# The feed-forward turn in the order gate, gate, value, value, way back, with the values copied out of PSUM by ScalarE

## The reference, cut to what matters

```python
def conv_ffn(xn, w_in, conv_w, conv_b, w_out, rows):
    a, v = _split(xn @ w_in, (D_FF, D_FF))
    if rows is None:
        a = dwconv_seq(a, conv_w[1])
    else:
        a = dwconv_grid(a, conv_w, rows)
    h = jax.nn.gelu(a + conv_b) * v
    return h @ w_out
```

## Time and profile before

| | us |
|---|---|
| median of three runs | 3967.95 (3964.62 to 3971.0) |
| span of the profiled execution | 3966.6 |
| TensorE matmul busy | 3448.7 (87% of the span) |
| VectorE busy | 1854.5 (47%) |
| GpSimd busy | 968.1 (24%) |
| ScalarE busy | 736.0 (19%) |

### The profile page before, as it was taken

The page is one execution under the profiler, slowest core; times in us unless marked ns, Lnnn a source line. Parts: engine busy times, 40 slices in busy tenths (PEclk is TensorE's granted clock), DMA queues, the critical chain, the costliest instruction groups (busy, mean ns, idle before and its releaser), DMA issues. The chain is left out here.

```text
span 3966.6 us, 49337 instructions
## 1 busy us (share of the span) xinstructions
PE 3448.7 (87%) x19579; PEld 3332.8 (84%) x19579; DVE 1854.5 (47%) x2483; ACT 736.0 (19%) x1381; POOL 968.1 (24%) x435
## 2 busy tenths in 40 slices
PE   8899999969799999999978889886868888888885
PEld 8788899959799999999977778776868888888885
DVE  2333332230755554555554244253365566655555
ACT  1333321121300010000004233232120000000000
POOL 1111122203123333333221212111212333233330
PEclk8898999979899999999988899898989999999997
DMA  3111121132211111111131010112310010110102
GB/s 155 39 52 51 51 74 51 61 101 73 86 54 57 59 69 58 63 53 53 53 105 56 27 42 24 38 36 79 112 39 32 32 37 33 36 37 32 37 32 96
DMA packets 86088, 225.58 MB, mean 57 GB/s; under 512 B 8000, under 2 KB 45120, under 8 KB 85872
## 3 DMA queue, kind: packets, MB, share of 16 engines
q1 hardware_dynamic: 44064, 163.16, 11.9%
q10 hardware_dynamic: 41936, 61.17, 4.5%
HBM read 193.89 MB, written 30.41 MB: 57 GB/s over the span
## 5 line engine op out<-in xcount | busy, mean ns | idle before, releaser
L712 PE MATMUL bank<-xh,wh 128*128 128x384 f32 x3888 | 1378.2, 354 | 225.3 <-DVE cc L2116 141.7
L712 PE MATMUL bank<-xl,wh 128*128 128x384 f32 x3888 | 1350.3, 347 | 0.0
L712 PE MATMUL bank<-xh,wl 128*128 128x384 f32 x3888 | 1346.1, 346 | 0.0
L693 POOL TENSOR_TENSOR wh<-raw,ones 128x1024 fp32r<-128x1024 f32 x206 | 420.2, 2040 | 2893.2 <-PE bank L712 1831.6
L712 PEld LDWEIGHTS bank<-xh,wh 128*128 128x128 f32 x3888 | 771.6, 198 | 258.5 <-DVE cc L2116 124.4
L712 PEld LDWEIGHTS bank<-xl,wh 128*128 128x128 f32 x3888 | 770.9, 198 | 0.5
L712 PEld LDWEIGHTS bank<-xh,wl 128*128 128x128 f32 x3888 | 768.7, 198 | 0.0
L2108 DVE SCALAR_TENSOR_TENSOR cc<-pad,cw,cc 128x1024 f32<-128x1024 f32 x352 | 573.8, 1630 | 6.9
L695 POOL TENSOR_TENSOR wl<-raw,wh 128x1024 fp32r<-128x1024 f32 x206 | 542.8, 2635 | 16.2
L712 PE MATMUL bank<-hh,wh 128*128 128x384 f32 x1056 | 373.0, 353 | 69.8 <-DVE y L2138 32.2
L2138 DVE TENSOR_TENSOR y<-y,bank 128x384 f32<-128x384 f32 x480 | 247.1, 551 | 278.1 <-PE bank L712 256.3
(11 more groups left out here) (231 smaller groups left out, 2622.2 us busy)
## 6 DMA issues: line engine op xcount, KB each, us to landing
raw<-in_w SPq DMA_DIRECT2D x206, 512.0 KB, 3.3
ada_w<-in_ada SPq DMA_DIRECT2D x80, 512.0 KB, 3.4
residual_scratch<-y ACTq DMA_DIRECT2D x9, 1536.0 KB, 5.9
xg<-residual_scratch ACTq DMA_DIRECT2D x9, 1536.0 KB, 7.9
xr<-mixer_scratch ACTq DMA_DIRECT2D x16, 576.0 KB, 3.8
front<-in_ada SPq DMA_DIRECT2D x16, 512.0 KB, 8.1
y<-in_x SPq DMA_DIRECT2D x1, 4608.0 KB, 19.6
mixer_scratch<-hout ACTq DMA_DIRECT2D x24, 192.0 KB, 1.9
```

The lines of the kernel that those rows point to most:

```text
L693: nc.gpsimd.tensor_tensor(wh[s][:, :], raw[s][:, :], ones[:, 0:1].broadcast_to([128, 1024]), ALU.mult).then_inc(w_hi[s], 1)
L712: return nc.tensor.matmul(out, lhsT, rhs, start=start, stop=stop)
```

## The change

TensorE's turn becomes gate 0, gate 1, value 0, value 1, and then the way back of the pair before; the host's order of the blocks and SyncE's pattern follow. ScalarE pads both gate tiles, and copies each value tile out of the three pj banks into a new SBUF tile `vs`, which frees the banks; `vs0` and `vs1` lie over tiles that only the norms use. VectorE does the 12 taps of tile 0, the 12 of tile 1, both products (now one instruction of 1152 elements each, from SBUF), then the 24 additions of the way back, then both parts hl. ScalarE writes hh once the way back, which reads the old hh, is over.

```diff
-            stream("ffn_b", FP - 1, "wawwwawawa")
+            stream("ffn_b", FP - 1, "wawawawaww")
...
                 with n.loop(pe, f"pe.ffn{layer}", FP - 1):
-                    project_all(slot())
-                    if with_ada:
-                        ada(0)
-                    down()
-                    for j in range(1, 4):
+                    for j in range(4):
                         project_all(slot())
                         if with_ada:
                             ada(j)
+                    down()
...
-            def dve_takes(s):
-
-                for c in range(2):
-                    n.next(pj_full[c])
+            def values(t, s):
+
+                for c in range(3):
+                    job(s, c)
+                    fn(vs[t][:, tg(c)], pj[c][:, 0:TG], COPY).then_inc(pj_free[c], 1)
                     n.next(pj_free[c])
-                n.next(w_used[s])
-                n.next(pj_free[2])
+                fn(tickw[:, t:t + 1], eps[:, :], COPY).then_inc(v_ready, 1)
...
             def upper(t):
-                act.wait_ge(pj_free[2], n.before(pj_free[2]))
+                act.wait_ge(h_ready, n.next(h_ready))
                 fn(hh[:, t, :], cc[t][:, :], COPY).then_inc(hh_ready, 1)
 
             def pair(with_down):
                 pads(0, slot())
+                pads(1, slot())
+                gelu(0)
+                values(0, slot())
+                gelu(1)
+                values(1, slot())
                 if with_down:
                     for _ in range(2):
-                        n.next(w_used[slot()])
-                gelu(0)
-                dve_takes(slot())
+                        s = slot()
+                        act.wait_ge(w_used[s], n.next(w_used[s]))
                 upper(0)
-                pads(1, slot())
-                gelu(1)
-                dve_takes(slot())
                 upper(1)
...
-            def value(t, s):
+            def value(t):
 
                 dve.wait_ge(gelu_done, n.next(gelu_done))
-                for c in range(3):
-                    full_ = w_used[s] if c == 2 else pj_full[c]
-                    dve.wait_ge(full_, n.next(full_))
-                    give(v.tensor_tensor(cc[t][:, tg(c)], cc[t][:, tg(c)], pj[c][:, 0:TG], ALU.mult), pj_free[c])
+                dve.wait_ge(v_ready, n.next(v_ready))
+                link(v.tensor_tensor(cc[t][:, :], cc[t][:, :], vs[t][:, :], ALU.mult), h_ready)
+
+            def rest(t):
                 dve.wait_ge(hh_ready, n.next(hh_ready))
...
                             give(v.tensor_tensor(dst, dst, mb[i][:, 0:TG], ALU.add), mb_free[i])
-                            if j % 2:
-                                conv_tap(0, j // 2)
...
             def pair(turn, with_down, column, saved=0):
                 set_taps(turn)
-                act_takes(slot())
+                for _ in range(4):
+                    act_takes(slot())
+                for t in range(2):
+                    for tap in range(12):
+                        conv_tap(t, tap)
+                value(0)
+                value(1)
                 if with_down:
                     down()
                 else:
-                    for tap in range(12):
-                        conv_tap(0, tap)
                     dve.wait_ge(x_saved, saved)
                     link(v.memset(y[:, :, :], 0.0))
-                value(0, slot())
-                act_takes(slot())
-                for tap in range(12):
-                    conv_tap(1, tap)
-                value(1, slot())
+                rest(0)
+                rest(1)
                 if column is not None:
                     conditioning(column)
```

More of the change, by code:

```diff
@@ L32 @@
               'conv_done': 2,
+              'h_ready': 2,
               'pj_free0': 4,
@@ L135 @@
               'mb_full3': 4,
-              'pj_free0': 2,
-              'pj_free1': 2,
-              'pj_free2': 2,
               'pj_full0': 4,
               'pj_full1': 4,
+              'v_ready': 2,
               'w_used0': 3,
@@ L398, in build @@
         tickv = sb("tickv", [128, 1])
+        tickw = sb("tickw", [128, 2])
         cond = sb("cond", [128, KT, 2])
@@ L427, in build @@
         ffn_scope = ExitStack()
+        values_scope = ExitStack()
+        vs = [sb(f"vs{t}", [128, T], scope=values_scope) for t in range(2)]
+        values_scope.close()
         sb("under_norm", [128, TG + KT * TG], scope=ffn_scope)
@@ L558, in build @@
             "conv_loaded a_padded conv_done gelu_done hh_ready hl_ready pads_clear")
+        v_ready, h_ready = sems("v_ready h_ready")
         mix_loaded, gates_logs, gates_rows, gates_exp, m_stored, cols_ready = sems(
@@ L2315, in ffn_blocks @@
     for p in range(FP):
-        blocks.append(a_(2 * p))
+        blocks += [a_(2 * p), a_(2 * p + 1), v_(2 * p), v_(2 * p + 1)]
         if p:
             blocks += down(p - 1)
-        blocks += [v_(2 * p), a_(2 * p + 1), v_(2 * p + 1)]
     return blocks + down(FP - 1)
```

## The result

The changed kernel takes 3715.3 us (median of four runs, 3711.9 to 3722.93); the kernel before took 3969.07 us in the same comparison. The ratio is 0.936, 95% interval 0.9347 to 0.9374. The forecast was 3714 us.

A forecast was written before the change was run, and what follows sets the result against it. TensorE bounds the kernel, losing 15.8 us a turn in layer 1 and 6.3 in layer 0. Savings of 175.2 and 79.2 us take 3966.6 to 3712.2; plus 1.35 for the median, told as 3714, range 3698 to 3748.

The forecast's parts named there:

- The length of a turn: TensorE's loop turn: 75.3 us in layer 1 and 82.4 in layer 0, where it was 91.0 and 88.8.
- The schedule inside a turn of layer 1: After TensorE ends gate 0: all taps over at 36 us (33 to 39), second product over at 40.8.
- The cover of 0.3 us: In layer 1's way back, the first addition frees bank mb0 at 41.4 us; TensorE's fifth group needs it at 41.7.
- The port: VectorE's product from SBUF shares ports with GpSimd's splits; if wl also went first, it would end at 43.2 us, costing 2.1.
- The third rival: TensorE's granted clock falls to 0.918 in the unbroken turns of both layers: 3855 us, chance 4%.
- The first rival: VectorE comes late to the additions of the way back, so TensorE waits there: 3735 to 3756 us, chance 17%.
- the prediction's own sign: The forecast is wrong if a turn of layer 1 takes more than 78 us or the clock falls in it.
- Weights: Each weight block is still split during TensorE's next block; layer 0 keeps 2.7 us of cover, so no wait.
- the second: Rival: conditioning transfers hold the weights in layer 0 and nothing is gained there: 3793 us, chance 4%.
- the fourth rival: VectorE's taps in a row keep GpSimd from splitting weights, 16.3 us in each of 20 turns: 4040 us, chance 2%.
- The last restarts: Before each layer's last way back TensorE waits for hh and hl: 7.2 us, once per layer, where 12.84 and 9.82 before.
- the start of layer 1: First pair: clearing y (7.74 us) moves behind the products and is covered; TensorE goes on at 2926.2 instead of 2936.41.

The follow-up runs named there:

- the thirds: The changed kernel with hh and hl made in six instructions of 384 columns each, the last way back starting per token group: 3716.9 us, ratio 0.9365.
- the order alone: The changed kernel without ScalarE's copies: VectorE multiplies out of the pj banks, product 0 ahead of the taps of tile 1; 3859.9 us, ratio 0.972.
- one copy: The changed kernel with only value 0 copied to SBUF; VectorE multiplies value 1 out of the pj banks in three instructions: 3710.8 us, ratio 0.9346.
- y cleared early: The changed kernel with VectorE clearing y between the two products in each layer's first pair, instead of behind them: 3703.8 us, ratio 0.9326.

## Why the prediction was right

- The length of a turn: 75.3 and 82.4 us forecast, 75.1 and 82.0 measured. The way of reading it, blocks of 12.48 us and groups of 1.056 where nobody holds TensorE, was good to 0.4 us.
- The schedule inside a turn of layer 1: taps over at 36, second product at 40.8, forecast; 35.8 and 40.7 measured. The cover of 0.3 us was real: 0.8 us of delay of the additions already made TensorE wait 0.5 us in each turn. Part of this is luck: the 36 rests on 16.2 us for the taps of tile 1, a value half way between two rows, and they took 15.9.
- The port: that a VectorE instruction with two SBUF inputs is served in turn with GpSimd's is seen at the second product (2.24 us against 1.36), behind wh and ahead of wl, which takes 3.40 us there; with a PSUM operand in its place the product takes 1.49 us and wl 2.40. The rule of the Trainium skill ("SBUF — State Buffer", section "SBUF: two separate sides"), exclusive for a whole instruction, also tells what the thirds did, and the trace agrees: the wait falls by a quarter only, since a small instruction (1.81 us beside wh, 0.56 alone) waits for wh too.
- The clock: 1.00 in turns of 75 us one behind the other, nine in layer 1. The third rival, less clock in unbroken work, did not come.
- The first rival, late additions, came in one turn only, the first of layer 1: 83.1 us with a clock of 0.50 behind the wait. By the prediction's own sign (more than 78 us, or the clock falls) that turn is a miss, in the other nine it holds.
- Weights: no wait of TensorE for GpSimd or for a transfer in either feed-forward part; the second and the fourth rival did not come.
- The last restarts: 7.2 us of wait each, measured 6.7.
- The term that was mis-sized is the start of layer 1: I put the clearing of y behind the products as covered. It is covered for TensorE's projections, but VectorE starts the taps of the first turn 7.2 us after gate 0 in place of 0.6, with 0.3 us of cover: 5.7 us of wait and some 2 with the slow clock. Between the restarts 2020.68 and 3886.16 lay 1865.5 us, and now 1696.9: a gain of 168.6, where I had 175.2. Layer 0 gave 82.7 where I had 79.2, since its turns are 0.4 us shorter; what follows the last restart gave 0.9. The sum, 252.2 for 254.4, is thus close partly because two errors have opposite signs.

What I did not forecast is how the gain divides. In the new order, by the experiments, ScalarE's copy of value 0 is the main part (149 us between the order alone and one copy; it also lets product 0 stand behind all taps), the place of the taps comes next (75 us with the copies there), and the copy of value 1 is nearly free of effect. In the old order no run takes the two copies apart; there it is the banks of value 1 that the next gate 0 needs.

## What to carry to other kernels

Work out how long one turn is where nobody holds the busiest engine, then walk through the turn to the first time at which each bank must be back; the mean share of a second engine says nothing of whether it is in time. A copy that frees a bank pays where the next projection needs that bank; where other banks come next, it can be left out. Look at the first and the last turn apart, since what is covered in the steady turn may come late there.

## What the runs showed of the hardware that was not expected

The 24 groups of a way back came 1.04 us apart in some turns and 1.06 in others, with the clock at 1.00 and no wait: the additions of the kernel after in two turns that follow each other.

```profile
3234.75 0.56 DVE L2141 TENSOR_TENSOR y<-y,bank 128x384 f32<-128x384 f32 x1 [0.49 <-PE bank L717]
3235.78 0.55 DVE L2141 TENSOR_TENSOR y<-y,bank 128x384 f32<-128x384 f32 x1 [0.48 <-PE bank L717]
...
3309.78 0.55 DVE L2141 TENSOR_TENSOR y<-y,bank 128x384 f32<-128x384 f32 x1 [0.51 <-PE bank L717]
3310.84 0.55 DVE L2141 TENSOR_TENSOR y<-y,bank 128x384 f32<-128x384 f32 x1 [0.51 <-PE bank L717]
```

In that kernel turns of 75.0 and 75.4 us alternate for most of layer 1; with thirds, or with y cleared early, all behind the first have 75.0, and with one copy all have 75.4. It is worth up to 4 us for ten turns. What decides it stays open: no run was made for it.

And a wait of TensorE costs more than its own length. Behind those of 3.4, 5.7, 6.4, 6.7 and 7.7 us the records show the clock at 0.50. Where turns can be compared, those with 3.4 us of wait were 5.5 us longer, the one with 5.7 was 8.1 longer, those with 6.4 were 8.5 longer, and those with 7.7 were 10.2 longer, so 2.1 to 2.5 us more than the wait each time. Turns with 0.5 us of wait were 0.6 us longer, at a clock of 1.00.
